# Stick-breaking attention as a suffix product instead of a sum of logarithms, with a new table of ranks

## The reference, cut to what matters

```python
def block(args):                      # one block of 128 queries
    logits = jnp.einsum('bqhd,bkhd->bhqk', qi, kf) * scale
    mask = key_pos[None, :] < q_pos[:, None]
    log_keep = jnp.where(mask, jax.nn.log_sigmoid(-logits), 0.0)
    later = lax.cumsum(log_keep, axis=3, reverse=True) - log_keep
    weights = jnp.where(mask, jnp.exp(jax.nn.log_sigmoid(logits) + later), 0.0)
    return jnp.einsum('bhqk,bkhd->bqhd', weights, vf)
```

## Time and profile before

| | |
|---|---|
| time, median of 3 | 2294.95 us (2293.42 to 2296.1) |
| span of the profiled execution | 2291.9 us |
| mean granted TensorE clock | 0.995 |
| TensorE busy | 2247.2 us, 98% |
| VectorE, ScalarE, GpSimd busy | 1594.7, 1112.9, 1030.9 us |
| share of the chain that ended last | PE 84%, DVE 8%, ACT 2%, issue 2%, DMA 2% |

### The profile page before, as it was taken

One profiled execution on the slowest core, in us unless ns is written; L12 is line 12 of the kernel. 1 busy time (PEld: TensorE's weight loads), 2 busy tenths in 40 slices (PEclk: granted clock), 3 DMA queues, 4 the chain that ended last, 5 costly groups with the idle time before them and its releaser, 6 DMA issues.

```text
span 2291.9 us, 31262 instructions
## 1 busy us (share of the span) xinstructions
PE 2247.2 (98%) x11389; PEld 1785.5 (78%) x11389; DVE 1594.7 (70%) x2217; ACT 1112.9 (49%) x2008; POOL 1030.9 (45%) x643
## 2 busy tenths in 40 slices
PE   9999989999999999999999999999999999999999
PEld 6778867677878888887887777777777888888886
DVE  7865768776596554689449798888888655545745
ACT  5554157674364555444446365645433322225553
POOL 2212245444247666657767211111123765556663
PEclk9999999999999999999999999999999999999999
DMA  4113353344325443955452301111123343338554
GB/s 160 40 44 99 122 177 107 98 139 158 109 93 188 161 152 133 314 173 166 143 170 83 124 29 46 47 46 47 56 79 124 134 143 111 111 133 294 183 171 147
DMA packets 153764, 289.43 MB, mean 126 GB/s; under 512 B 34915, under 2 KB 44387, under 8 KB 153612
## 3 DMA queue, kind: packets, MB, share of 16 engines
q1 hardware_dynamic: 153612, 287.44, 38.3%
HBM read 207.88 MB, written 79.51 MB: 125 GB/s over the span
## 4 chain that ended last, share of the span: by engine, by line
PE 84%; DVE 8%; ACT 2%; issue 2%; DMA 2%; POOL 1%; SPq 0%; DVEq 0%; POOLq 0%; ACTq 0%
PE bank L869 12%; PE bank L871 12%; PE bank L867 12%; PE bank L639 12%; PE bank L643 11%; PE bank L641 11%; PE bank L716 2%; PE bank L932 2%; PE bank L963 1%; PE bank L945 1%; ACT t L1005 1%; DVE t L1434 1%; DVE t L1974 1%; PE bank L836 1%; PE bank L854 1%
## 5 line engine op out<-in xcount | busy, mean ns | idle before, releaser
L2100 POOL TENSOR_TENSOR t<-t,t 128x512 fp32r<-128x512 f32 (+1 forms) x494 | 810.5, 1652 | 1068.3 <-ACT t L1005 1062.1
L1005 ACT ACTIVATE t<-t 128x512 fp32r<-128x512 f32 (+1 forms) x689 | 448.3, 676 | 653.5 <-PE bank L871 276.3
L639 PE MATMUL bank<-t,t 128*128 128x512 f32 x1360 | 548.5, 403 | 0.0
L643 PE MATMUL bank<-t,t 128*128 128x512 f32 x1360 | 531.4, 391 | 1.1 <-DVE t L1434 0.6
L641 PE MATMUL bank<-t,t 128*128 128x512 f32 x1360 | 530.1, 390 | 1.7 <-POOL t L2100 1.7
L867 PE MATMUL bank<-t,t 128*128 128x512 f32 x1316 | 514.2, 391 | 6.2 <-DVE t L1818 4.6
L869 PE MATMUL bank<-t,t 128*128 128x512 f32 x1316 | 513.3, 390 | 1.4 <-POOL t L2100 1.4
L871 PE MATMUL bank<-t,t 128*128 128x512 f32 x1316 | 513.1, 390 | 0.7 <-DVE t L1434 0.7
L639 PEld LDWEIGHTS bank<-t,t 128*128 128x128 f32 x1360 | 255.7, 188 | 62.7 <-issue 12.7
L643 PEld LDWEIGHTS bank<-t,t 128*128 128x128 f32 x1360 | 255.3, 188 | 58.3 <-POOL t L2100 1.3
L641 PEld LDWEIGHTS bank<-t,t 128*128 128x128 f32 x1360 | 255.9, 188 | 56.3 <-issue 4.6
(11 more groups left out here) (250 smaller groups left out, 2641.2 us busy)
## 6 DMA issues: line engine op xcount, KB each, us to landing
t<-in_w SPq DMA_DIRECT2D x87, 512.0 KB, 3.6
hid_scr<-t SPq DMA_DIRECT2D x112, 256.0 KB, 2.1
t<-hid_scr SPq DMA_DIRECT2D x112, 256.0 KB, 2.7
t<-in_wf SPq DMA_DIRECT2D x80, 256.0 KB, 3.3
t<-in_wf SPq DMA_DIRECT2D x36, 512.0 KB, 4.5
g_scr<-t SPq DMA_DIRECT2D x36, 512.0 KB, 2.9
t<-g_scr SPq DMA_DIRECT2D x72, 256.0 KB, 3.4
t<-in_wo SPq DMA_DIRECT2D x24, 512.0 KB, 3.6
```

Source lines behind the costliest of these rows:

```text
L639: e.matmul(ps[:, :], hi[:, w, :], XH[:, x, hs], start=k == 0, stop=False)
L643: last = e.matmul(ps[:, :], hi[:, w, :], XL[:, x, hs], start=False, stop=k == j.nk - 1)
L1005: return e.activation(out, in_, ACT.Copy, **kw)
L2100: return e.tensor_tensor(out, x, high.bitcast(F32), ALU.subtract)
```

## The change

The stick-breaking weights are made as a product. `sg` takes the place of `smin` and `se`: ScalarE writes sigmoid(logit) from the bank to a buffer `odds`, and 1 minus it to a buffer `keep` that holds a whole query block. `ss` is now one reversed scan with multiply on VectorE, in place in `keep`, that starts from the next piece's first column instead of a separate carry. A new GpSimd step `sw` multiplies `odds` by `keep` shifted by one column. `sx` is gone. The bank of the logits is free after the first instruction of `sg`; `odds` is double, and is free for piece n + 2 once piece n is transposed. In the program the table `SHIFT` is another one too, and since it sets the order of all engines, steps change places in stages that the product does not touch, the first DMAs among them. Names in it that no longer exist (`smin`, `sx`) do nothing. SP's first DMAs were `wload(0)`, `c0`, `x(0, 0)`, `x(1, 0)`, `x(2, 0)`, `x(3, 0)`, `wload(1)`; they are now `x(2, 0)`, `wload(1)`, `wload(0)`, `c0`, `x(0, 0)`, `x(1, 0)`, `x(3, 0)`; ScalarE now makes `whi(1)` ahead of `whi(0)`, and GpSimd `wlo(1)` ahead of `wlo(0)`. The new order's activation tables are loaded 15 times as before, one of them (for the sigmoids) at the first `sg` instead of at 1727 us.

```diff
-SHIFT = {("abias",): 1.5, ("apv", 1): 1.25, ("atr", 3): -1.5, ("bg", 1): -1, ("bm2", 0): -0.25, ("bm2", 1): 3, ("cR", 1): 1.75, ("co", 0, 4): -2,
...
+SHIFT = {("abias",): 1, ("am", 0, 0, 2): 2.25, ("apv", 1): 0.5, ("aq", 0): 3.5, ("aqk", 5, 3): 1, ("atr",): -2, ("bel", 0): -1, ("bel", 0, 2): 1.75,
...
+         ("tx", 2): -4, ("tx", 3): -8, ("wc", 1, 9): 1.75, ("whi", 25): 9.25, ("wload", 1): -2.5, ("x", 2): -2, ("x1l", 1): 2.5, ("x2h",): 8,
@@ class Memory
-        self.e2, self.m2, self.w2 = (many(o, 4, 2, [128, S]) for o in (169, 177, 185))
+        self.odds, self.keep = many(169, 4, 2, [128, 2, 512]), [many(177 + 8 * a, 4, 2, [128, S]) for a in range(2)]
@@ def sl
-            q.wait_ge(*[done("ss", a, *K.piece_before(n, 2)) for a in range(2)])
+            q.wait_ge(*[part("sg", (a, *K.piece_before(n, 2)), 1) for a in range(2)])
@@ def scalar_engine
-    def se(a, i, p_):
+    def sg(a, i, p_):
+
         qb, k0, k1 = PIECES[p_]
-        x = M.stick_buffer("e", a, p_ % 2, k1 - k0)
-        q.wait_ge(done("smin", a, i, p_))
-        e.activation(x, x, ACT.Exp).then_inc(*tick("se", a, i, p_))
-        q.wait_ge(part("se", (a, i, p_), 1))
-        e.activation(x, x, ACT.Ln, bias=one_c).then_inc(*tick("se", a, i, p_))
-
-    def sx(a, i, p_):
...
+        n, odds = 12 * i + p_, M.odds[a][:, p_ % 2, 0:k1 - k0]
+        q.wait_ge(done("sl", i, p_))
+        if n >= 2:
+            i0, p0 = K.piece_before(n, 2)
+            q.wait_ge(*[done("st", i0, PIECES[p0][0], g) for g in K.groups(p0)])
+        e.activation(odds, banks[2 + 2 * a + p_ % 2][:, 0:k1 - k0], ACT.Sigmoid).then_inc(*tick("sg", a, i, p_))
+        q.wait_ge(part("sg", (a, i, p_), 1))
...
+        e.activation(M.keep[a][qb % 2][:, k0:k1], odds, ACT.Identity, scale=-1.0, bias=one_c).then_inc(*tick("sg", a, i, p_))
@@ def vector_engine
-    def smin(a, i, p_):
...
-        tt(m_, x, ps[:, 0:nk], ALU.max).then_inc(*tick("ss", a, i, p_))
-        q.wait_ge(part("ss", (a, i, p_), 1))
-        e.tensor_tensor_scan(x[:, ::-1], one_c.broadcast_to([128, nk]), m_[:, ::-1], 0.0, ALU.mult, ALU.add).then_inc(*tick("ss", a, i, p_))
...
-        stt(w, x, -1.0, ps[:, 0:nk], ALU.mult, ALU.add).then_inc(*tick("ss", a, i, p_))
+        keep = M.keep[a][qb % 2]
+        q.wait_ge(done("sg", a, i, p_))
+        if k1 < 128 * (qb + 1):
+            q.wait_ge(done("ss", a, i, p_ - 1))
+        x = keep[:, k0:k1][:, ::-1]
+        start = keep[:, k1:k1 + 1] if k1 < 128 * (qb + 1) else 1.0
+        e.tensor_tensor_scan(x, x, one_c.broadcast_to([128, k1 - k0]), start, ALU.mult, ALU.mult).then_inc(*tick("ss", a, i, p_))
@@ def gpsimd_engine
+    def sw(a, i, p_):
+
+        qb, k0, k1 = PIECES[p_]
+        n = min(k1, 128 * qb + 127) - k0
+        odds = M.odds[a][:, p_ % 2, 0:n]
+        q.wait_ge(done("ss", a, i, p_))
+        e.tensor_tensor(odds, odds, M.keep[a][qb % 2][:, k0 + 1:k0 + 1 + n], ALU.mult).then_inc(*tick("sw", a, i, p_))
@@ def second_layer
-            add("pe", "sv", i, p_, rank=3)
+            add("pe", "sv", i, p_, rank=3, behind=[("sv", K.piece_before(12 * i + p_, 1))] if i or p_ else ())
```

57 lines of the change are left out of this document (17 added, 40 removed), and 18 rows, old and new, of tables (SHIFT, SIGNALS).

## The result

The changed kernel takes 2316.98 us (median of 4 runs, 2312.91 to 2321.6) against 2294.77 us for the kernel before in the same comparison: a ratio of 1.0095, 95% interval 1.0081 to 1.011. It is slower by 22 us where 4.7 us faster was forecast. The profiled execution is its fastest, with a span of 2311.1 us, 19.2 more than before.

A forecast was written before the change was run, and what follows sets the result against it. TensorE, busy for 98% of the span, was taken as the bound, so only its waits and clock could move. The terms 1.5 - 4.6 - 3.1 + 1.5 = -4.7 gave 2290.2 us from 2294.95, range 2281 to 2302 for 8 in 10.

The forecast's parts named there:

- the rest: Tables, tail and all other places: order differences move by tenths, covered by TensorE's matmuls; put at nothing.
- fsum(1): Around 623 to 660 us: new wait of 3.0, wait at 656.0 shrinks to about 1.6, half clock goes; -3.1 us.
- The product: Stick stage: 12 tight pieces wait 4.2 us for weights, 2.7 given back; +1.5 us, bounds -2.7 and +12.7.
- The delta rule at 452 us: `cs(1, 4)` moves ahead of reductions and `as1`: wait of 2.90 and 1.7 of half clock go; -4.6 us.
- The start: First transfers reordered: first useful matmul at about 11.1 us, wait for `wlo(1)` goes; +1.5 us, bounds +1.1 and +2.8.
- The wait at 318.8: Delta rule, `lb(1, 0, 1)`: the 5.19 us wait stays, bound by the load of `aq(0)`; 0, bounds -7.5 and +2.
- rival B: Level: the gain at `cs(1, 4)` is eaten by the next wait behind it; 2294.9 us, chance 0.30.
- Rival A: Stick stage: VectorE-GpSimd lock makes 12 tight pieces each wait a product more; +12.7, 2301.5 us, chance 0.24.

The follow-up runs named there:

- vector_product: The product form under the old order table, with the product `sw` made by VectorE instead of GpSimd: 2288.8 us, ratio 0.9969 to the kernel before.
- product_only: The changed kernel with the old order table, so only the product form is new: 2292.51 us, ratio 0.9986 to the kernel before.
- before_fsum: The kernel before with one move on TensorE, `fsum(1)` ahead of `fa(0, 0)` and `fa(1, 0)`: 2299.97 us, ratio 1.0014.
- old_start: The changed kernel with the old order table up to bulk job 45, first transfers included: 2307.97 us, ratio 1.0053 to the kernel before.
- old_chain: The changed kernel with old table entries in the delta rule for all steps but the attention's: 2307.23 us, ratio 1.0047 to the kernel before; stage 229.4 us.
- after_all: The changed kernel with three places of the delta rule put back together: 2314.89 us, ratio 1.0081 to the kernel before; delta rule 238.9 us.
- after_fill: The changed kernel with unread matmuls put into three TensorE waits of the delta rule's first chunk: 2312.47 us, ratio 1.0075 to the kernel before.

## Why the prediction was wrong

The step that failed is the last of the sum: outside of the places that it read, the new order was put at nothing ("the rest", with "TensorE's matmuls as the cover"). In the delta rule, where no bulk matmuls cover anything, it cost 11.2 us. The terms for `fsum(1)` and for `cs(1, 4)` failed too. One by one:

**What bounds the kernel.** TensorE, as said. But the step "TensorE waits for 2.7 us in the whole stage, and this is the most that the lighter VectorE can give" is false. vector_product took 5.7 us off the stage, and product_only 2.4, with as much idle time as before (4.1 against 3.7 us over the whole of it), so that idle time is not the bound. Where the 2.4 us come from is open. A modelled end of 0.39 us for a matmul that is followed after 0.23 can hide a wait of up to 0.16 us (my estimate), and the order of TensorE's steps differs: an `sl` follows an `st` in 21 places before and in 8 in product_only, at 0.23 and 0.20 us each.

**The product, +1.5.** Measured -0.3 in the changed kernel, and -2.4 with the old table. The waits for the weights came near the forecast in size, and with its cause:

```profile
PE bank L944 <- POOL t L2187: 3.9, 6, 1.5
```

6 places, 3.9 us, against 12 places and 4.2, and the bounds held. That the total is near is in part luck, since half the places waited twice as long. The price at the scan was too high: in the changed kernel the scans of 512 columns take 1.45 us in the mean, and 5 of the 48 take over 2 us, where 2 to 2.5 was to be seen at each of the 24 of head 1. The hold-up of VectorE by GpSimd was seen but priced at the wrong place: up to 3.3 us of the stage go by it (vector_product), 0.5 of them at the weights and 2.7 at VectorE's other work. The Trainium skill ("SBUF — State Buffer", section "SBUF: two separate sides") states that the two share a port pair as an exclusive lock, which a VectorE instruction with two SBUF inputs needs against a GpSimd one that reads SBUF. The traces agree: line 1944 took 2284 ns beside the products and 1225 without. The Trainium skill ("Perfetto Trace Analysis", section "Optimizing Scalar/DVE Operations") warns that moving work between the two might not help. The runs agree: with the product on VectorE the kernel is 3.7 us faster.

**The delta rule at 452 us, -4.6.** Wrong; the gain is nil. The wait at `cR(1, 5)` is gone in the changed kernel, but `cT(0, 5)`, ahead of it, waits 3.55 us for VectorE, and 3.4 us of half clock follow as before. This is the prediction's rival B, which has the right place and far too small a price for the rest of the stage. The reading failed at the question why `cs(1, 4)` was late before. VectorE's timeline of the kernel before shows what the prediction passed over:

```profile
447.90 1.23 DVE L1636 TENSOR_TENSOR t<-t,t 128x8 f32<-128x8 f32 x1
449.17 1.18 DVE L1638 TENSOR_SCALAR t<-t 128x8 f32<-128x8 f32 x1
450.26 0.15 DVE L1639 TENSOR_TENSOR t<-t,t 128x8 f32<-128x8 f32 x1
```

Eight columns in 1.23 us, beside GpSimd's three instructions from 446.15 to 450.31; the first two of `as1` end within 0.04 us of the end of one of them, 449.11 and 450.31. `as1` was not much work in front of `cs`, it was held up. What stands in front of `cs` in the new order, `qkm(0, 6)` and `gn(0, 4)`, has the same kind of operands and meets the two `ap(4)`, 3.1 us each. The prediction took the instructions of the front's order listing as free because their durations alone are short.

**`fsum(1)`, -3.1.** Wrong in sign: +3.3 for the stage in the changed kernel, +3.7 for the whole of before_fsum. The failed step is "`fa(0, 1)` is bound by VectorE's `fc11` at the same time as before". `fc11(0)` needs results of TensorE's `fa` steps, which all came later by the wait for `fsum(1)`, so the wait in front of `fa(0, 1)` stayed at 4.65 us there. In the changed kernel it shrank to 1.39, but `fsum(1)` waited 4.74 instead of 3.0, because `hac(3, 1, 7)` and a step in front of it took 1.75 us each beside GpSimd, and the sum of the two is 1.5 us more than before. Of the half clock 3.4 us went, worth 1.7, as the forecast had hoped in part. The rest of the 3.3 came behind `fa(0, 1)`, where the forecast had nothing, with new waits of 0.41 us for VectorE at 687.21 and 1.09 for GpSimd's low part of a weight at 700.70. A small misreading besides: the 1.12 us at 625.20 are one addition and not two.

**The start, +1.5.** The useful matmuls began at 10.69 (forecast 11.1). The term is 3.5 us in the profile, above its bound of 2.8. The step that failed is "that goes, -1.9, since its tile is now loaded first": the wait for `wlo(1)` is gone, but GpSimd makes `wlo(1)` ahead of `wlo(0)`, and the second matmul waits for the second of them, to 12.57.

```profile
7.39 5.12 POOL L2080 TENSOR_TENSOR t<-t,t 128x1024 fp32r<-128x1024 f32 x2 [6.95 <-ACT t L1004]
```

The third waits 0.72 us more for VectorE's low part of x, and half clock follows for 3.4 us. With what it does to the clock later the start is worth 9.0 us (old_start).

**The wait at 318.8, and "the rest", 0.** Here is the error that decides. At 318.8 the wait of 5.19 for `lb(1, 0, 1)` went, and waits of 1.72, 3.07 and 1.32 us came for `co(0, 0)`, `cR(0, 1)` and `aqk(0, 0)`, with 10.2 us of half clock instead of 6.8. The delta rule was read at two places where TensorE had waited, and the many other differences in its order, over the five engines, were put at nothing. It became 11.2 us longer. By the profiled executions 2.8 us of these are more idle time, and the busy time at half clock rose from 8.0 to 22.5 us, worth 7.2; 1.2 us are in neither. old_chain tells that the chain's entries bring it, and after_all that it is not in the three places with the longest waits. In the later stages "other places move by tenths" was 1.8 us.

**Rivals and range.** Rival A, the slow one, had the right sign and the wrong cause. None of the rivals was "the order is worse where nothing waits now", and so the range ended 15 us too low. Two of rival A's sums do not come out of its own terms, without weight for the result: with 12 places late by 0.8 us the whole is +0.7 (not +2.2), and by 1.0 it is +3.1 (not +4.6).

**Open.** Why half clock comes where it does. It followed waits in most places, but old_start has the waits of 340 us without it, after_fill has it after waits were filled, and the runs of one kernel differ (changed kernel: mean clock 0.988 to 0.992, 2321.6 to 2312.9 us).

## What to carry to other kernels

A change that comes with a new order for all engines is two changes; price the order first, stage by stage, and where a stage is a tight chain over several engines don't put its unexamined moves at zero but at a spread of both signs, several us here. Before moving a step out from behind others, ask why those took long: one held up by GpSimd will be followed by the next one that is. Work with two operands in SBUF that leaves VectorE for GpSimd may not be gone from VectorE: here its price showed at VectorE's other work.
